# Expert weights loaded by slot count instead of by step, and one running count of loaded experts, in a two-layer MoE trunk kernel

## The reference

```python
expert_id = g_idx * EXPERTS_PER_GROUP + e_idx        # 16 experts, 2 per token
gates = jnp.sum(jax.nn.one_hot(expert_id, N_EXPERTS) * weights[..., None], axis=1)
a = jnp.einsum('td,edf->tef', t, w_gate)             # per expert 1024 x 256
u = jnp.einsum('td,edf->tef', t, w_up)               # per expert 1024 x 256
hid = jax.nn.silu(a) * u * gates[..., None]
y = jnp.einsum('tef,efd->td', hid, w_down)           # per expert 256 x 1024
```

## Time and profile before

| what | value |
|---|---|
| median of 3 runs | 1569.82 us (1565.95 to 1572.94) |
| profiled execution, its own time | 1566.19 us |
| its span | 1564.0 us |
| PE busy | 1291.1 us, 83% of the span |
| DVE, ACT, POOL busy | 45%, 27%, 15% |
| granted TensorE clock, mean | 0.916 |
| HBM read, written | 217.17 MB, 28.38 MB |

### The profile page before, as it was taken

How to read it: one execution, slowest core, us unless ns; L and a number is a source line. 1 busy time by engine, 2 the same in 40 slices (tenths; PEclk the granted TensorE clock), 3 DMA queues, 4 the chain that set the end, 5 groups by cost and what they waited for, 6 DMA issues and landing times.

```text
span 1564.0 us, 23096 instructions
## 1 busy us (share of the span) xinstructions
PE 1291.1 (83%) x8094; PEld 772.6 (49%) x8094; DVE 700.5 (45%) x1655; ACT 418.9 (27%) x961; POOL 228.5 (15%) x358
## 2 busy tenths in 40 slices
PE   4999978999999589878478998799999945986950
PEld 3455455777676444333244454477776733532420
DVE  0445414777544624232346443277664444332326
ACT  2110146666401101010121113466661100100112
POOL 3310121000110012210211101200002001110023
PEclk8899979999999689999879999899999966998985
DMA  9500576000314844999470015900004073299943
GB/s 337 201 13 1 201 279 169 2 2 28 120 43 148 308 168 111 356 381 381 180 265 13 1 44 177 317 3 2 16 14 149 28 270 107 83 355 382 366 166 149
DMA packets 132759, 247.53 MB, mean 158 GB/s; under 512 B 6688, under 2 KB 80672, under 8 KB 128512
## 3 DMA queue, kind: packets, MB, share of 16 engines
q1 hardware_dynamic: 111264, 175.39, 32.9%
q0 software_dynamic: 21344, 70.08, 12.5%
HBM read 217.17 MB, written 28.38 MB: 157 GB/s over the span
## 4 chain that ended last, share of the span: by engine, by line
PE 42%; DVE 7%; DMA 7%; issue 5%; SPq 3%; DVEq 1%; POOL 1%; ACT 1%; POOLq 0%; ACTq 0%
PE ps L2022 8%; PE ps L1743 7%; PE ps L1641 5%; PE ps L1919 4%; PE ps L2067 4%; PE ps L2016 3%; PE ps L1799 3%; PE ps L1852 3%; DMA ring<-in_moe_w_up 2%; DMA ring<-in_w_mod 2%; SPq L502 2%; PE ps L2060 2%; DVE ring L1276 1%; DMA h_rows<-work 1%; DMA hT_region<-h_rows,idx 1%
## 5 line engine op out<-in xcount | busy, mean ns | idle before, releaser
L1743 PE MATMUL ps<-ring,hT_region 128*128 128x512 f32 (+1 forms) x640 | 268.5, 576 | 1.7 <-ACT hT_region L903 1.7
L1276 DVE TENSOR_SCALAR_CACHE_REDUCE ring<-ps 128x768 f32<-128x768 f32 (+1 forms) x168 | 132.7, 820 | 157.5 <-PE ps L1799 102.2
L1743 PEld LDWEIGHTS ps<-ring,hT_region 128*128 128x128 f32 x640 | 120.5, 191 | 132.1 <-issue 131.3
L962 ACT ACTIVATE ring<-ring,negm 128x768 f32<-128x768 f32 (+1 forms) x168 | 137.7, 820 | 31.8 <-DVE ring L1276 31.8
L2022 PE MATMUL ps<-ring,hT_region 128*128 x304 | 139.3, 612 | 7.8 <-DVE hT_region L1583 4.9
L1919 PE MATMUL ps<-ring,hT_region 128*128 128x384 f32 (+1 forms) x480 | 141.8, 453 | 0.0
L1799 PE MATMUL ps<-arena,qT 64*128 64x384 f32 (+1 forms) x640 | 124.8, 507 | 13.5 <-DVE ring L1276 6.0
L1606 DVE COPY work<-ps 128x256 f32<-128x256 f32 x29 | 12.3, 424 | 223.6 <-PE ps L1641 223.6
L1919 PEld LDWEIGHTS ps<-ring,hT_region 128*128 128x128 f32 x480 | 89.8, 190 | 44.1 <-issue 0.7
L1852 PE MATMUL ps<-work,arena 128*64 128x128 f32 x1600 | 105.6, 278 | 6.6 <-ACT work L978 4.3
L2016 PE MATMUL ps<-ring,hT_region 128*64 x160 | 84.1, 686 | 32.4 <-issue 32.4
(11 more groups left out here) (303 smaller groups left out, 1712.5 us busy)
## 6 DMA issues: line engine op xcount, KB each, us to landing
ring<-in_w_mod SPq DMA_DIRECT2D x24, 2048.0 KB, 10.7
ring<-in_moe_w_gate SPq DMA_DIRECT2D x32, 1024.0 KB, 11.6
ring<-in_moe_w_up SPq DMA_DIRECT2D x32, 1024.0 KB, 13.5
arena<-in_moe_w_down SPq DMA_DIRECT2D x32, 1024.0 KB, 10.5
y_rows<-arena POOLq DMA_DIRECT2D x29, 512.0 KB, 6.5
ring<-in_w_in SPq DMA_DIRECT2D x6, 2048.0 KB, 18.7
arena<-mod_rows POOLq DMA_DIRECT2D x12, 512.0 KB, 6.8
h_rows<-work POOLq DMA_DIRECT2D x10, 512.0 KB, 3.0
```

The lines of the kernel that those rows point to most:

```text
L962: act.activation(v, v, ACT.Exp, bias=negm[:, 2 * (k % 3) + m:2 * (k % 3) + m + 1], scale=-1.0, accum_out=sums[:, c:c + 1]).then_inc(exp_do ...
L1276: ts(o_, i_, -pair_of(p)[4], None, ALU.mult, ALU.min, accum_out=col).then_inc(m_ready, 1)
L1743: last = mm(ps[:, b, 0:n], hT[:, c, t * P:(t + 1) * P], w[:, c, :], start=(c == 0), stop=(c == KC - 1))
```

## The change

SP's loads no longer go by steps. `steps_of(l, e)` reads from a new table `EI_DONE` how many steps are needed until expert e is done. Expert e (4 to 15) is loaded into its slot, now a constant address, once `gu_done` (for gate and up) or `dn_done` (for down) has reached that count for expert e-4. SP also waits itself for each expert's landing, in order of the experts, and adds one to `gu_loaded` or `dn_loaded`. TensorE waits for one of these counts, against a register from the table `EI_LAST` (the number of the last expert in the step, plus one). It reads four registers per step instead of two, and the ring and arena addresses come ready from tables. Before the loads of expert 2, SP waits for the first gather of rows of that layer. DVE writes other tables; GpSimd's memsets of `slot_step` go.

```diff
+            def steps_of(l, e):
+                return sp.value_load(experts_i[0:1, EI_DONE + e:EI_DONE + e + 1], min_val=1, max_val=N_ET)
+            def gate_up_of(l, e):
+                if e >= RING:
+                    sp.wait_ge(gu_done[l], steps_of(l, e - RING))
+                gate_up_weights(l, l * NE + e, slot[LATE[e % RING]], wgu_landed[e % RING])
+            def down_of(l, e):
+                if e >= RING:
+                    sp.wait_ge(dn_done[l], steps_of(l, e - RING))
+                at = DN0 + 2048 * LATE[e % RING]
+                down_weights(l, l * NE + e, arena[:, at:at + 2048], wd_landed[e % RING])
+            def pass_on(signal, l, e, landed, n):
+                sp.wait_ge(landed[e % RING], n * (NE // RING * l + e // RING + 1))
+                sp.sem_inc(signal[l], 1)
             for g, (kind, l, i, at) in enumerate(USES):
                 if kind == "moe":
+                    if i == 2:
+                        sp.wait_ge(s_hg[l][0], 16)
                     slot_free(g)
-                    gate_up_weights(l, l * NE + i, to, wgu_first[i])
+                    gate_up_of(l, i)
...
                     if i == RING - 1:
                         sp.wait_ge(experts_ready, l + 1)
-                        for step in range(2, N_ET + 1):
-                            if step < N_ET:
-                                gate_up_of_step(l, step)
-                            if step > 2:
-                                down_of_step(l, step - 1)
+                        for e in range(2, NE + 2):
+                            if RING <= e < NE:
+                                gate_up_of(l, e)
+                            pass_on(gu_loaded, l, e - 2, wgu_landed, 32)
+                            if RING <= e - 1 < NE:
+                                down_of(l, e - 1)
+                            pass_on(dn_loaded, l, e - 2, wd_landed, 16)
...
@@ dve tables
-                ts(r_two[row, :], two[row, :], r_incl[row, NE - 1:NE], None, ALU.is_lt, ALU.add,
-                   accum_out=r_used[row, :])
+                b8 = r_wide[row, 0:NE * N_ET].rearrange("p (e i) -> p e i", e=NE)
+                tt(b8, r_incl[row, :].unsqueeze(2).to_broadcast([1, NE, N_ET]),
+                   two[row, :].unsqueeze(1).to_broadcast([1, NE, N_ET]), ALU.is_gt)
...
+                red(r_ends[row, :], b8, AX.X, ALU.add)
+                red(r_last[row, :], b6[:, 1:N_HALF:2, :], AX.X, ALU.add)
...
-                tt(b6, b6, slot_step[row, :].unsqueeze(1).to_broadcast([1, N_HALF, NE]), ALU.mult)
-                red(r_at[row, :], b6, AX.X, ALU.add)
...
@@ tensor
                 def gate_up(i):
-                    form[i] = pe.value_load(experts_i[0:1, EI_FORM + i:EI_FORM + i + 1], min_val=0, max_val=2)
-                    a_at[i] = pe.value_load(experts_i[0:1, EI_A + i:EI_A + i + 1], min_val=0, max_val=RING - 1)
+                    form[i], last_e[i], at_ring, at_arena[i] = (
+                        pe.value_load(experts_i[0:1, k + i:k + i + 1], min_val=lo, max_val=hi)
+                        for k, lo, hi in ((EI_FORM, 0, 2), (EI_LAST, 1, NE), (EI_RING, 0, (RING - 1) * 4096),
+                                          (EI_ARENA, DN0, DN0 + (RING - 1) * 2048)))
                     with if_used(pe, i):
...
+                        pe.wait_ge(gu_loaded[l], last_e[i])
...
                 def down(i):
                     with if_used(pe, i):
...
+                        pe.wait_ge(dn_loaded[l], last_e[i])
```

More of the change, by code:

```diff
@@ L44 @@
 MIN_ET = -(-N_PAIR // P)
-EI_SLOT, EI_NEW, EI_A, EI_FORM, EI_USED = N_HALF, 2 * N_HALF, 3 * N_HALF, 3 * N_HALF + N_ET, 4 * N_HALF
+EI_RING, EI_ARENA, EI_FORM, EI_LAST, EI_DONE = (N_ET * k for k in range(5))
+EI_USED = EI_DONE + NE
 N_SMALL_IN = 20
@@ L253, in trunk @@
         fac, negh = small[:, 39:55], small[:, 55:71]
-        slot_step = small[:, 124:140]
         by_step = lane_w[:, 0:64].rearrange("p (k n) -> p k n", k=2)
@@ L283, in trunk @@
         w_landed = [sem(f"w_landed{s}") for s in range(RING)]
[L285 to L288, removed]
+        wgu_landed = [sem(f"wgu_landed{e}") for e in range(RING)]
+        wd_landed = [sem(f"wd_landed{e}") for e in range(RING)]
+        gu_loaded = [sem(f"gu_loaded{l}") for l in range(DEPTH)]
+        dn_loaded = [sem(f"dn_loaded{l}") for l in range(DEPTH)]
         s_setup_dma = sem("s_setup_dma")
@@ L467, in trunk @@
         r_c, r_nt, r_incl, r_excl = rt(16), rt(16), rt(16), rt(16)
-        r_sl, r_tl, r_ex = rt(2 * NT), rt(2 * NT), rt(N_HALF)
-        r_at, r_one, r_two, r_used = rt(N_HALF), rt(N_HALF), rt(N_ET), rt(1)
+        r_sl, r_tl, r_ex = rt(2 * NT), rt(2 * NT), rt(1)
+        r_ends, r_last = rt(NE), rt(N_ET)
         r_par, r_lim, r_steps, r_le = rt(NE // 2), rt(NE), rt(2 * N_ET), rt(NE * NE)
@@ L538, in _ @@
                 if kind == "moe":
+                    if i == 2:
+                        sp.wait_ge(s_hg[l][0], 16)
                     slot_free(g)
[L540 removed]
+                    gate_up_of(l, i)
                     if i == 0:
                         sp.wait_ge(wo_done, l * 15 + 15)
[L543 removed]
+                    down_of(l, i)
                     if i == RING - 1:
                         sp.wait_ge(experts_ready, l + 1)
[L546 to L550 removed]
+                        for e in range(2, NE + 2):
[5 more added lines that the diff above has]
+                            pass_on(dn_loaded, l, e - 2, wd_landed, 16)
                     continue
@@ L591, in _ @@
                       allow_small_or_imprecise_dtypes=True)
-            for e in range(RING):
-                pool.memset(slot_step[:, e:NE:RING], float(LATE[(e + 1) % RING] - LATE[e]))
             pool.iota(tok_id[:], pattern=[[P, NT]], base=0, channel_multiplier=1,
@@ L1537, in _ @@
                    iota_t[row, :].unsqueeze(2).to_broadcast([1, N_HALF, NE]), ALU.is_le)
-                ts(r_two[row, :], two[row, :], r_incl[row, NE - 1:NE], None, ALU.is_lt, ALU.add,
-                   accum_out=r_used[row, :])
+                b8 = r_wide[row, 0:NE * N_ET].rearrange("p (e i) -> p e i", e=NE)
+                tt(b8, r_incl[row, :].unsqueeze(2).to_broadcast([1, NE, N_ET]),
+                   two[row, :].unsqueeze(1).to_broadcast([1, NE, N_ET]), ALU.is_gt)
                 dve.drain()
-                red(r_ex[row, :], b6, AX.X, ALU.add)
-                ts(experts_i[row, EI_USED:EI_USED + 1], r_used[row, :], 0.0, None, ALU.add)
+                red(r_ends[row, :], b8, AX.X, ALU.add)
+                red(r_last[row, :], b6[:, 1:N_HALF:2, :], AX.X, ALU.add)
+                dve.drain()
+                cp(experts_i[row, EI_DONE:EI_DONE + NE], r_ends[row, :])
+                cp(experts_i[row, EI_USED:EI_USED + 1], r_ends[row, NE - 1:NE])
+                ts(experts_i[row, EI_LAST:EI_LAST + N_ET], r_last[row, :], 1.0, float(NE), ALU.add, ALU.min)
                 b8 = r_big[row, :].rearrange("p (i n) -> p i n", n=2 * NE)
@@ L1549, in _ @@
                     red(r_steps[row, k * N_ET:(k + 1) * N_ET], b9, AX.X, ALU.add)
-                dve.drain()
-                tt(b6, b6, slot_step[row, :].unsqueeze(1).to_broadcast([1, N_HALF, NE]), ALU.mult)
-                ts(r_ex[row, :], r_ex[row, :], float(NE - 1), None, ALU.min)
-                dve.drain()
-                red(r_at[row, :], b6, AX.X, ALU.add)
[L1555 to L1562, removed]
+                    dve.drain()
+                a_ = r_steps[row, 0:N_ET]
+                ts(experts_i[row, EI_RING:EI_RING + N_ET], a_, 4096.0, 4096.0 * LATE[0], ALU.mult, ALU.add)
+                ts(experts_i[row, EI_ARENA:EI_ARENA + N_ET], a_, 2048.0, DN0 + 2048.0 * LATE[0], ALU.mult, ALU.add)
+                ts(experts_i[row, EI_FORM:EI_FORM + N_ET], r_steps[row, N_ET:2 * N_ET], 2.0, None, ALU.add
+                   ).then_inc(experts_ready, 1)
                 dve.wait_ge(r_rows, l + 1)
@@ L2008, in gate_up @@
                             pe.wait_ge(mod_evac, (l + 1) * N_MOD + MOD_FIRST)
-                        wa = ring[:, bass.ds(pe.snap(a_at[i] * 4096), 4096)].rearrange("p (c n) -> p c n", c=KC)
+                        wa = ring[:, bass.ds(at_ring, 4096)].rearrange("p (c n) -> p c n", c=KC)
                         g = ps[:, 2 + i % 2, :]
@@ L2050, in down @@
                             pe.wait_ge(y_evac_a[l], i)
-                        wa = arena[:, bass.ds(pe.snap(a_at[i] * 2048 + DN0), 2048)].rearrange("p (c n) -> p c n", c=2)
+                        wa = arena[:, bass.ds(at_arena[i], 2048)].rearrange("p (c n) -> p c n", c=2)
                         h = hidT[i % 2]
@@ L2077, in _ @@
                 load_tiles_used(pe, l)
-                form, a_at = {}, {}
+                form, last_e, at_arena = {}, {}, {}
                 rows_T(0)
```

2 lines of the change are left out of this document (removed).

## The result

| | before | after |
|---|---|---|
| median | 1569.66 us (4 runs) | 1609.76 us (4 runs, 1606.44 to 1615.85) |
| ratio to before | | 1.0263, 95% interval 1.0231 to 1.0295 |
| profiled execution, its span | 1566.19, 1564.0 | 1609.11, 1607.0 |
| granted clock, mean | 0.916 | 0.909 |

The change makes the kernel 40 us slower; 1600 was forecast, with a range of 1571 to 1621. Cut into stretches, the two profiled executions stand against each other as follows. Every number is a difference of two starts in PE's, POOL's or SP's timeline.

The account below looks back on a forecast made before the run. Waits for weights and SP's issue time were taken to bound the two expert stages. Terms 17 - 4 + 12 + 5 = +30 on the profiled 1566.2 us, with the median 3.6 above it, gave 1600, range 1571 to 1621.

Parts of the forecast that it names:

- part 1: Expert stages: loads asked for earlier, experts 4, 5 and 6 move into the idle half; layer 0 keeps 7 to 17 us.
- The floor of 7 to 17 us: Layer 0 after step 7's gate-up: DMA needs 83 to 93 us, PE's own pace 75.7, so 7 to 17 stay.
- part 5: TensorE's two more register loads per step: 0.1 to 0.7 us at some 20 steps; in all +5 (0 to +12).
- Part 2: Late expert steps wait for SP's program order: layer 1 +12 (-5 to +18), layer 0 -4 (-16 to +5).
- the model sequence: Earlier trace's down, gate, up, down, gate, up, 1261.89 to 1273.59: 11.7 us, taken for layer 1's steps 8 and 9.
- The slow clock: After an idle stretch ahead of a step, the 1.2 GHz level for 5.1 us, costing 2.5 us each time.
- Part 3: Step 0 waits while SP issues experts 2 and 3: layer 0 +6.8, layer 1 +10.5, together 17 (9 to 22).
- Part 4: Routing arithmetic on DVE, ahead of the gather: 1.5 us off per layer (0.5 to 2), booked in the start.
- A: Faster rival: SP's issues stay short, start -4, chains 3.3 each; 1547 us, chance 0.12.
- B: No-change rival: start costs 17, layer 1's steps 8 and 9 wait 7.9, layer 0 gains 16; 1571, chance 0.09.
- C: Slower-by-less rival: start as forecast, middle even, chains at their short end; 1583 us, chance 0.16.
- D: Slower-by-more rival: POOL's traffic stretches the start (22) and the floors (+5, +18); 1622 us, chance 0.13.

Follow-up runs that it names:

- experiment 10: Only half the bytes of experts 8 to 15 loaded, against the changed kernel with SP's signals moved earlier: layer 0's gate-ups 171.7 us in place of 182.5.
- experiment 9: TensorE reads three registers per step in place of four, against the changed kernel with SP's signals moved earlier: 1538.97 us, ratio 0.9804.
- experiment 6: Two more unused register loads on TensorE in each gate-up, against the kernel before the change: 1578.35 us, ratio 1.0040.
- experiment 8: Only half the bytes of experts 2 and 3 loaded, against the changed kernel: six issues 7.4 us in place of 15.0; total time not usable.

## Why the prediction was right

- **What bounds it, and part 1.** The early half took up loads and the first stall of each layer went, as forecast. The floor of 7 to 17 us for layer 0 held: even with both signals moved, layer 0 has 182.5 - 165.2 = 17 us too many, and 11 of them go in experiment 10 with half of the late loads. The other 6 are no wait for loads (from step 2 on no step idles over 0.7 us there); part of them are the register loads of part 5, which 165.2 does not hold (experiment 9 gets 2.8 back).
- **Part 2, SP in the signal path.** Right in mechanism and place: the steps named (7, 8, 9, 10 in layer 1; 8 and 9 in layer 0) are those whose releaser is L527, together with layer 0's step 13 (1.05 us, the "little behind it" of the prediction) and step 11 (7.22 us), which I had left to the floor. For layer 1 the term was +12 and, with its share of part 5, some 14; it measured +19.6.

  Mis-sized are steps 8 and 9, where I had 11.6 us of idle each: it is 13.9 and 14.4, and their intervals are 29.2 and 28.8 us where I had announced 24 to 27. The held issues were not dearer than in the model sequence from 1261.89 on the earlier trace rows: that one has a down of 3.39 us and an up of 5.94, step 8's chain a down of 4.55 and an up of 3.69. What I left out lies between the issues: ahead of step 8 the gaps at 1438.2, 1440.2 and 1446.0, where SP reads registers and passes on signals, are 0.65, 1.28 and 0.66 us, 2.6 in all, and from the last issue to the gate-up it is another 0.7.

  The slow clock was priced about right: the intervals that begin with steps 7, 8 and 9, less the idle at their end and less 12.2, leave 3.2, 2.2 and 3.2 us, for 2.5 each, and after the starts of steps 7 and 9 the granted clock is 0.50 for 5 us. So of the 6 us missed in layer 1, idle time is 3, the clock 1, and the rest is spread over the other steps. Step 7 (3.0 idle for 4.4) and step 10 (2.65 for 3.3) were a little dear.

  One row was misread: the longest down issue of the kernel before took 7.52 us, not 5.8; no sum uses it. For layer 0 the term was -4, with part 5 about -2; it measured -3.6.
- **Part 3, the start.** Forecast was gate-up 0 at 15.2 us after the gather lands. In layer 0 it came 15.4 after, in layer 1 about 17. The gather took 4.4 and 4.3 us. The sum of both starts is +22.3 from the gather's issue; +17 was booked with DVE's saving of 3 in it, so 22.3 stands against 20.
- **Part 4, DVE.** From the first operation of the tables to `experts_ready` 7.5 us became 5.9: 1.6 for the forecast 1.5. The middle operations of 288 elements took 0.44 us:

```profile
534.32 0.74 DVE L1531 TENSOR_TENSOR work<-work,lane 1x576 f32<-1x576 f32 x1
534.99 0.44 DVE L1534 TENSOR_TENSOR hT_region<-work,lane 1x288 f32<-1x288 f32 x1
...
540.03 0.16 DVE L1553 TENSOR_SCALAR experts_i<-work 1x18 int32<-1x18 f32 x1
```

- **Part 5, register loads.** +5 forecast; experiment 6 measures +6.3 for two more loads in the kernel before, and experiment 9 gets 6.9 back by taking one away (6.7 in the stretches, though the intervals of the times overlap).
- **Not forecast.** 6.6 us of the profiled difference lie between the expert stages, in code that the change does not touch. That stretch took 538.9 to 549.2 us over the twelve profiled executions, one of each kernel. The changed kernel with both signals moved has 539.0 there, and the kernel before with two more register loads has 549.2, so the 6.6 do not follow the change; repeated traces of one kernel, which would prove it, there are none. The -1.4 at the very start is DVE's saving: its tables begin 0.2 us later and take 1.6 less. The stage terms give 8.5 - 3.6 + 13.8 + 19.6 + 0.1 = 38.4, and 37.0 with the -1.4, against 40 for the medians (36 to 46 by the interval of the ratio).
- **Rivals.** A needed SP not to be held; experiment 8 shows that it is held, and that the hold shrinks with the loads. The Trainium skill's rule ("DMA: Bandwidth & Descriptors", section "Issuing engines are not separate DMA queues") that starting a DMA is usually small beside it does not describe this queue when it is full: 4.1 to 4.5 us of SP's time for 1.05 MB, where down loads land 5.1 to 14.6 us after their issue in the changed kernel, 11.3 in the median. What A promised (1547) was there to be had, though not by A's way: two moved signals give 1545.85 with the issues as long as before. B and C needed chains at their short end, 7.9 us at layer 1's steps 8 and 9; they were 13.9 and 14.4. D (1622) had the start at 22 and layer 1 at +18, which is nearer to what was measured than the forecast, but layer 0 at +5, where it was -3.6. The 1600 came out 10 us low because two terms, layer 1's late half and the start, were too small; what was priced too dear (steps 7 and 10) is 2 us in all.

## What to carry to other kernels

When a queue both issues transfers and passes on "landed", price each signal by all that stands ahead of it in program order, the issues at their held length, and put it ahead of the next issue that waits for a late event. A stretch in which the consumer idles, the DMA engines are not full and the releaser is the issuing queue is a question of order, not of bandwidth. Waits by a static index are often wider than the data needs; look which they are before you delay a load.

## What the runs showed of the hardware

- SP's issue of a 1.05 MB load takes 0.34 to 0.7 us with little under way. A full down load right behind an up load, so with 2.1 MB or more issued just before, took 1.5 to 7.5 us (80 cases), a gate load right behind a down load 0.54 to 0.65 us in 49 of 54. Halving the loads halved the time of six issues (15.0 to 7.4 us).
- The first gather of layer 0 took 7.4 to 10.3 us with the loads of experts 2 and 3 queued beside it (four kernels) and 4.2 to 4.5 where they waited for it (eight).
- TensorE's register loads have a threshold in this kernel: a third one per step costs nothing (11.6 to 11.7 us per full step), a fourth shows (12.0). That fits the lead of TensorE's sequencer, about 1.1 us before the array by the prediction's working, and 0.64 for each load.
- Code that no edit touches took up to 10 us more in one of these executions than in another. In the changed kernel the granted clock stands at 0.50, the 1.2 GHz level, for the 10 us from 965 shown above; in the kernel before it is 0.83 in the piece that resembles it most:

```profile
960.00:970.00 10.00, 7.28 (x96) 4.82 (x96) 3.17 (x20) 5.08 (x20) 0.00 (x0) 0.83 0.01 2
```
